# Causal and strict masks of two attentions: added by VectorE on the diagonal block, or by an identity product on TensorE

## The chip, the cores and the metric

The kernel runs on one core of one Trainium2 chip. Its time is the device time of one execution in microseconds; a comparison takes the median of several executions. Everything is computed in fp32.

## The reference, cut to what matters

Two transformer blocks follow each other on 512 tokens of width 1024. The first block (windowed attention, convolution, a mixture of experts) is not touched. The second block has two attentions of 8 heads of 64, a projection, and a layer that gathers 128 rows of a table of experts for each token (8 heads, 16 experts a head):

```python
def forgetting_attention(q, k, v, log_fcum):          # "fox"
    ...
        logits = jnp.einsum('bhqd,bhkd->bhqk', qb, k, ...) * scale
        logits = logits + fq[..., :, None] - log_fcum[..., None, :]
        mask = k_pos[None, :] <= q_pos[:, None]
        logits = jnp.where(mask, logits, -jnp.inf)
        p = jax.nn.softmax(logits, axis=-1)

def stick_breaking_attention(q, k, v):                # "stick"
    ...
        mask = k_pos[None, :] < q_pos[:, None]
        log_beta = jax.nn.log_sigmoid(z)
        log_one_minus = jnp.where(mask, jax.nn.log_sigmoid(-z), 0.0)
        rest = lax.cumsum(log_one_minus, axis=3, reverse=True) - log_one_minus
        a = jnp.where(mask, jnp.exp(log_beta + rest), 0.0)

def peer_layer(h, w_query, sub_keys, expert_down, expert_up):
    ...
        u = expert_down[eb]
        act = jax.nn.gelu(jnp.einsum('td,thkd->thk', xb, u), approximate=False) * gb
        vv = expert_up[eb]
        return jnp.einsum('thk,thkd->td', act, vv)
```

## The kernel before

Each engine has its own program, written out by hand, and semaphores tie them together. The 512 queries are four tiles of 128. A unit `n` of an attention is one head and one tile `t` (`unit(n)`), over the keys of tiles 0 to `t`, so a unit works on 128 x `(t + 1) * 128` scores. There are 32 units of each attention. Units 0 to 7 are tile 0 of the eight heads ("the first part"); units 8 to 31 are tiles 1, 2, 3 of each head ("the second part").

The first part runs between the projections of the second block (`project2`, matmuls of L1969 and L1975): eight stick units, then eight fox units, one beside each projection. Then tile 0 goes through the output projection, the norm and its query, and the first top-16 selections are made.

The second part runs beside the expert layer. That layer is 32 steps (tile by head) of 8 parts; a part has two dot products of gathered rows on VectorE (`dot`, L1918), a piece of the top-16 selection for two steps later (`topk_part`), gelu and scaling on ScalarE (`coefs`, L1316 and L1318), and sums on TensorE (`up_sums`, L2595). GpSimd issues one gather for each of 16 experts a step (L885); a gather waits for its buffer (`pair_free`, given by TensorE after `up_sums`), and there are 8 buffers in the first 8 steps and 11 after. The list `PLAN` lays the attention's steps (`attend(s)`) behind the parts of the first six steps, in the same order on all engines, with 6 steps ahead of the first part. Stick units come first, then fox units, then output norm (`out_norm`), output projection, norm and queries of tiles 1 to 3. From step 8 on only the expert layer runs.

A stick unit: TensorE makes scores in a bank (`stick_scores`, L2436), ScalarE makes the softplus part `x` (`stick_soft`, L1177 to L1179), VectorE makes `x`, `y` and zeroes `x` on and above the diagonal (`stick_beta`, L1726, L1727, L1729, the last giving `sbb_done`), TensorE sums `x` over later keys into the same bank (`stick_sums`, L2444 and L2446) and adds the strict mask `stick_neg` there with a product of `ident` (L2448, giving `sbr_pe`), VectorE adds the bank to `y` (`stick_rest`, L1736), ScalarE takes the exponential, TensorE multiplies with the values (`stick_out`, L2460).

A fox unit: TensorE makes scores (`fox_scores`, L2392), adds the keys' decay (L2393) and adds the mask `causal` with a product of `ident` (L2394, giving `s_done`); VectorE takes the maximum (`fox_max`, L1750 and L1751), ScalarE the exponential (`fox_exp`, L1214), TensorE transposes (L2402), ScalarE copies (`fox_T`, L1223), TensorE multiplies with the values (L2412).

Both masks are 128 x 128 fp32 tiles in SBUF. A matmul of 128 x 128 fp32 stands in the trace as two rows. `link` on VectorE makes each of its instructions wait for the one before to be done.

Of the kernel before, what the change touches and what calls it, by code (L numbers as in the profile page):

```python
# [21 lines left out]
ALU = mybir.AluOpType  # L22
# [3 lines left out]
P = 128  # L26
# [6 lines left out]
H = 8  # L33
# [46 lines left out]
def build(nc, A, out):  # L80
    with ExitStack() as ctx:
        def sb(name, shape, dt=F32):
            return ctx.enter_context(nc.sbuf_tensor(name, shape, dt))

        def sem(name):
            return ctx.enter_context(nc.semaphore(name))
# [5 lines left out]
        bank = [ctx.enter_context(nc.psum_tensor(f"bank{i}", [P, 512], F32)) for i in range(8)]  # L92
# [24 lines left out]
        ident = sb("ident", [P, P])  # L117
        before = sb("before", [P, P])
        ones = sb("ones", [P, P])
        later_neg = sb("later_neg", [P, P])  # L120
        ones_neg = sb("ones_neg", [P, P])
        causal = sb("causal", [P, P])
# [6 lines left out]
        stick_neg = band_t[:, :, :].rearrange("p a b -> p (a b)")  # L129
# [124 lines left out]
        fcumT = arena_w[0:H, 4352:4352 + T]  # L254
# [135 lines left out]
        s_done = sem("s_done")  # L390
# [197 lines left out]
        def unit(n):  # L588
            return (n, 0, 0) if n < H else ((n - H) // NT[1], 1 + (n - H) % NT[1], 1)
# [9 lines left out]
        def stick_bank(n):  # L599
            return bank[1 + n % 3] if n < H else bank[(1, 2, 3, 7)[n % 4]]  # L600
# [37 lines left out]
        def slab(n):  # L638
            return slot(n % RING, *slabs[n][1])
# [737 lines left out]
        def _(dve):  # L1377
            link = Link(dve, dve_step)
# [340 lines left out]
            def stick_beta(n):  # L1719
                h, t, part = unit(n)  # L1720
                w = (t + 1) * P
                x, y, z = stick_x[part][n % 3], stick_y[part][n % len(stick_y[part])], stick_bank(n)
                dve.wait_ge(sbl_done, n + 1)
                if n >= len(stick_y[part]):
                    dve.wait_ge(sbo_pe, n + 1 - len(stick_y[part]))
                link(dve.scalar_tensor_tensor(out=x[:, 0:w], in0=z[:, 0:w], scalar=0.0, in1=x[:, 0:w], op0=ALU.max, op1=ALU.add))  # L1726
                link(dve.tensor_tensor(y[:, 0:w], z[:, 0:w], x[:, 0:w], ALU.subtract))  # L1727

                link(dve.tensor_tensor(x[:, t * P:w], x[:, t * P:w], before[:, :], ALU.mult), sbb_done)  # L1729

            def stick_rest(n):
# [6 lines left out]
            def stick_step(k, first):  # L1738
                part = int(first > 0)
                if of_part(k - REST[part], first):  # L1740
                    stick_rest(k - REST[part])
                if of_part(k - BETA[part], first):
                    stick_beta(k - BETA[part])

            def fox_max(n):
                w = (unit(n)[1] + 1) * P
                dve.wait_ge(s_done, H * TT + n + 1)
                if n >= 3:
                    dve.wait_ge(p_done, H * TT + n - 2)
                link(dve.tensor_reduce(smx[:, n % 3, 0:1], bank[1 + n % 3][:, 0:w], AX, ALU.max))  # L1750
                link(dve.tensor_scalar(smx[:, n % 3, 2:3], smx[:, n % 3, 0:1], -1.0, None, ALU.mult), nmax_done)  # L1751
# [11 lines left out]
            def fox_step(k, first):  # L1763
                part = int(first > 0)
                if of_part(k, first):
                    fox_max(k)
                if of_part(k - FOX_OUT[part], first) and last_of_head(k - FOX_OUT[part]):
                    fox_out(k - FOX_OUT[part])
# [196 lines left out]
        def _(pe):  # L1965
            def project(dst, w, at, rhs, chunks=DC, stationary=None):

                for c in range(chunks):
                    mm = pe.matmul(dst, w[:, c, at], rhs[:, c, :], start=(c == 0), stop=(c == chunks - 1))  # L1969
                return mm  # L1970

            def rows_of(dst, xT, t, w, at, chunks=DC):

                for c in range(chunks):
                    mm = pe.matmul(dst, xT[:, c, t * P:(t + 1) * P], w[:, c, at], start=(c == 0), stop=(c == chunks - 1))  # L1975
                return mm
# [28 lines left out]
            for c in range(DC):  # L2005
                if c % 2 == 0:
                    slab_ready(pe, N_MOD + c // 2)
                for j in range(4):
                    mm = pe.matmul(bank[0][32 * j:32 * j + 2, :], cvec[:, 0:2, c], slab(N_MOD + c // 2)[:, c % 2, T * j:T * j + T],
                                   start=(c == 0), stop=(c == DC - 1))  # L2010
# [7 lines left out]
            for c in range(DC):  # L2018
                for half in range(2):
                    mm = pe.matmul(bank[1][64 * half:64 * half + 64, 4 * c:4 * c + 4].rearrange("p (k r) -> p k r", k=2),  # L2020
                                   modr[:, c:T:DC], pick[:, :, 32 * half:32 * half + 2], start=True, stop=True)
# [36 lines left out]
            for m in range(18):  # L2058
# [6 lines left out]
                dst = bank[4 + m % 4]  # L2065
                if m < 4:
                    mm = project(dst[:, :], slab(N_K), slice(m * P, (m + 1) * P), hT)
                elif m < 8:
                    mm = project(dst[:, 0:CTX], slab(N_K), slice((m - 4) * P, (m - 3) * P), hcT)
                elif m < 10:  # L2070
                    mm = rows_of(dst[:, :], hcT, m - 8, slab(N_V), slice(0, 512))
                elif m < 14:
                    mm = rows_of(dst[:, :], hT, m - 10, slab(N_V), slice(0, 512))
                else:
                    mm = project(dst[:, :], slab(N_Q), slice((m - 14) * P, (m - 13) * P), hT)
                mm.then_inc(proj_done, 1)
                if m in PROJ_JOB:
                    j = PROJ_JOB.index(m)
# [50 lines left out]
            for i in range(PU + 3):  # L2129
# [10 lines left out]
                if i in AT_JOB:  # L2140
                    j = 3 + AT_JOB.index(i)
# [9 lines left out]
            for c in range(DC):  # L2151
# [9 lines left out]
                n = N_GA if c < 4 else N_GA + 4  # L2161
# [223 lines left out]
            def fox_scores(n):  # L2385
                h, t, part = unit(n)
                w = (t + 1) * P
                if n >= 3:
                    pe.wait_ge(p_done, H * TT + n - 2)
                at = slice(HD * (h % 2), HD * (h % 2) + HD)  # L2390
                dst = bank[1 + n % 3]
                pe.matmul(dst[:, 0:w], fqT[at, h // 2, t * P:(t + 1) * P], fkT[at, h // 2, 0:w], start=True, stop=False)  # L2392
                pe.matmul(dst[:, 0:w], ident[0:H, h:h + 1].broadcast_to([H, P]), fcumT[:, 0:w], start=False, stop=False)  # L2393
                pe.matmul(dst[:, t * P:w], ident[:, :], causal[:, :], start=False, stop=True).then_inc(s_done, 1)  # L2394

            def fox_transposes(n):
                h, t, part = unit(n)
# [18 lines left out]
            def fox_step(k, first):  # L2416
                part = int(first > 0)
                if k == first:
                    pe.wait_ge(sbc_done, UNITS if part else H)
                    pe.wait_ge(sbo_done, 1 + H if part else 1)  # L2420
                if of_part(k, first):
                    fox_scores(k)
                if of_part(k - FOX_T[part], first):
                    fox_transposes(k - FOX_T[part])
                if of_part(k - FOX_OUT[part], first):
                    fox_weighted(k - FOX_OUT[part])
# [13 lines left out]
            def stick_sums(n):  # L2440
                h, t, part = unit(n)
                x, dst = stick_x[part][n % 3], stick_bank(n)
                pe.wait_ge(sbb_done, n + 1)
                pe.matmul(dst[:, 0:(t + 1) * P], later_neg[:, :], x[:, 0:(t + 1) * P], start=True, stop=False)  # L2444
                for k in range(1, t + 1):
                    pe.matmul(dst[:, 0:k * P].rearrange("p (j q) -> p j q", q=P), ones_neg[:, :],  # L2446
                              x[:, k * P:(k + 1) * P].unsqueeze(1).broadcast_to([P, k, P]), start=False, stop=False)
                mm = pe.matmul(dst[:, t * P:(t + 1) * P], ident[:, :], stick_neg, start=False, stop=True)  # L2448
                mm.then_inc(sbr_pe, 1)

            def stick_out(n):
# [11 lines left out]
            def stick_step(k, first):  # L2463
                part = int(first > 0)
                if of_part(k, first):
                    stick_scores(k)
                if of_part(k - SUMS[part], first):
                    stick_sums(k - SUMS[part])
                if of_part(k - OUTS[part], first):
                    stick_out(k - OUTS[part])  # L2470
# [25 lines left out]
            for half in range(2):  # L2496
                pe.wait_ge(mixed_done, half + 1)
                for k in range(AC):
                    mm = pe.transpose(bank[1 + half][:, k * P:(k + 1) * P], mixed[0][half][:, 0, k * P:(k + 1) * P], ident[:, :])
# [144 lines left out]
            for n in range(TT * H):  # L2644
                t = n // H
# [53 lines left out]
```

## Time and profile before

| | us |
|---|---|
| median of 3 runs | 2970.42 |
| lowest and highest | 2962.66 and 2971.54 |
| the profiled execution | 2969.21 |
| its span, first to last instruction | 2967.4 |
| TensorE busy | 2264.3 (76%) |
| VectorE busy | 1420.9 (48%) |
| ScalarE busy | 758.9 (26%) |
| mean granted clock of TensorE, of full speed | 0.867 |

The page lists busy time, 40 slices of the span (about 74 us each), DMA queues, the chain of work that ended last and the costliest groups. PE is TensorE's matmuls, PEld its weight loads, DVE VectorE, ACT ScalarE, POOL GpSimd. In the views by window, "(x)" is a count of instructions, PEclk the granted clock as a share of 2.4 GHz, and DMA the busy share of 16 DMA engines. Times of the trace are us from the start of the span; L2394 is a line of the kernel.

### The profile page before, as it was taken

To read this page: it belongs to the slowest core of one execution; us is meant where nothing else is said; L and a number is where in the kernel's file an instruction comes from. 1 tells how busy PE (TensorE), PEld (TensorE's weight loads), DVE (VectorE), ACT (ScalarE), POOL (GpSimd) and SP (SyncE) were. 2 spreads that over 40 slices of the span, in tenths; PEclk is the share of its full clock that TensorE was granted. 3 is DMA by queue.
4 is the path that set the end of the run, shared out by engine and by line. 5 is a ranking of instruction groups with operands and counts; after the bars stand their busy time and mean duration, and the time that the engine had idled before them with its cause. 6 is when DMAs were issued, how large, how long until landed. Compare 5 with 4: busy or idle time off the path is not lost. (4 is left out here: it accounts for less than half of the span.)

```text
span 2967.4 us, 28984 instructions
## 1 busy us (share of the span) xinstructions
PE 2264.3 (76%) x9828; PEld 967.2 (33%) x9828; DVE 1420.9 (48%) x3332; ACT 758.9 (26%) x1753; POOL 591.3 (20%) x587
## 2 busy tenths in 40 slices
PE   5997899987777775799988978867755655565554
PEld 2543444532222222755655443322211111111110
DVE  2575411410000001301377667667678777777765
ACT  3104301110000001312177653222222222222212
POOL 0000000010000001000112223344344433443442
PEclk9999999989998997799998889888777777778786
DMA  9168429589999996512447868899999999999996
GB/s 340 60 240 291 167 79 211 206 318 400 404 402 399 398 399 245 182 57 84 147 175 288 307 262 320 359 411 416 417 421 422 421 421 421 421 404 421 421 421 253
DMA packets 213260, 922.17 MB, mean 311 GB/s; under 512 B 18986, under 2 KB 58968, under 8 KB 121230
## 3 DMA queue, kind: packets, MB, share of 16 engines
q0 software_dynamic: 78864, 552.72, 45.9%
q1 hardware_dynamic: 124480, 359.15, 33.0%
q10 hardware_dynamic: 9790, 8.73, 0.9%
q8 instruction: 65, 1.06, 0.1%
q14 instruction: 61, 0.50, 0.0%
HBM read 888.78 MB, written 31.77 MB: 310 GB/s over the span
## 5 line engine op out<-in xcount | busy, mean ns | idle before, releaser
L2595 PE MATMUL bank<-ring,arena_w 128*32 128x512 f32 x1568 | 604.1, 790 | 310.8 <-ACT arena_w L1318 310.6
L885 POOL DMA_INDIRECT ring<-in_expert_pair,ids x392 | 414.9, 1058 | 1048.6 <-PE bank L2595 680.1
L1969 PE MATMUL bank<-arena_h,ring 128*128 128x128 f32 (+2 forms) x1264 | 363.3, 448 | 10.3 <-DMA ring<-in_w_in 7.9
L2249 PE MATMUL bank<-ring,arena_h 128*64 128x512 f32 x1056 | 271.1, 672 | 88.0 <-DMA ring<-in_w_exp_up 83.2
L2595 PEld LDWEIGHTS bank<-ring,arena_w 128*32 128x32 f32 x1568 | 104.6, 128 | 657.6 <-ACT arena_w L1318 467.4
L1918 DVE CUSTOM_DVE_ANT_0 ring<-ring,arena_h 128x1024 f32<-128x1024 f32 x203 | 244.9, 1225 | 80.4 <-DMA ring<-in_expert_pair,ids 48.6
L1918 DVE CUSTOM_DVE_ANT_0 ring<-ring 128x1024 f32<-128x1024 f32 x189 | 229.6, 1224 | 79.7 <-DMA ring<-in_expert_pair,ids 71.3
L1969 PEld LDWEIGHTS bank<-arena_h,ring 128*128 128x128 f32 x1264 | 204.1, 196 | 160.3 <-issue 127.3
L1316 ACT ACTIVATE arena_w<-arena_w 128x2 f32<-128x2 f32 x256 | 51.8, 202 | 769.7 <-DVE arena_w L1918 769.3
L1641 DVE TENSOR_TENSOR arena_q<-arena_q,bank 128x256 f32<-128x256 f32 x32 | 13.5, 421 | 484.3 <-ACT arena_q L1060 484.3
L2249 PEld LDWEIGHTS bank<-ring,arena_h 128*64 128x64 f32 x1056 | 91.9, 155 | 264.9 <-issue 259.5
L2595 PE MATMUL bank<-arena_h,arena_w 128*32 128x512 f32 x200 | 131.3, 794 | 24.8 <-ACT arena_w L1318 24.8
L1318 ACT ACTIVATE arena_w<-arena_w 128x32 f32<-128x32 f32 x512 | 136.4, 313 | 8.4
L2262 PE MATMUL bank<-ring,arena_q 128*64 128x512 f32 x528 | 120.6, 598 | 19.9 <-DVE arena_q L1644 19.3
L2595 PE MATMUL bank<-pair_last,arena_w 128*32 128x512 f32 x140 | 97.3, 836 | 40.7 <-ACT arena_w L1318 40.7
L864 POOL DMA_INDIRECT arena_v<-ys_d,slot_i x8 | 8.9, 1106 | 564.8 <-SPq L716 554.5
L2595 PE MATMUL bank<-arena_v,arena_w 128*32 128x512 f32 x140 | 93.2, 804 | 31.8 <-ACT arena_w L1318 31.8
L1060 ACT ACTIVATE arena_q<-bank 128x256 f32<-128x256 f32 x32 | 12.3, 384 | 323.5 <-PE bank L2249 323.5
L1316 ACT ACT_TABLE_LOAD x63 | 80.8, 1283 | 50.6 <-DVE arena_w L1918 49.7
L1455 DVE SCALAR_TENSOR_TENSOR arena_x<-arena_x,convc 128x512 f32<-128x512 f32 x120 | 90.2, 752 | 4.3
L1975 PE MATMUL bank<-ring,arena_h 128*128 128x512 f32 x192 | 88.4, 618 | 0.0
L1524 DVE TENSOR_TENSOR arena_w<-bank,arena_w 128x512 f32<-128x512 f32 x8 | 8.3, 1036 | 154.8 <-ACT arena_w L1022 154.8
(472 smaller groups left out, 3040.8 us busy)
## 6 DMA issues: line engine op xcount, KB each, us to landing
ring<-in_w_exp_gate SPq DMA_DIRECT2D x33, 2048.0 KB, 19.4
ring<-in_w_exp_up SPq DMA_DIRECT2D x33, 2048.0 KB, 23.8
ring<-in_w_exp_down SPq DMA_DIRECT2D x33, 2048.0 KB, 24.9
ring<-in_w_in SPq DMA_DIRECT2D x15, 2048.0 KB, 20.2
ring<-in_w_mod SPq DMA_DIRECT2D x12, 2048.0 KB, 19.3
ring<-in_w_ada SPq DMA_DIRECT2D x12, 2048.0 KB, 14.7
xs_d<-zeros SPq DMA_DIRECT2D x1, 12032.0 KB, 70.8
ys_d<-arena_h ACTq DMA_DIRECT2D x64, 128.0 KB, 7.3
```

What stands on the lines that cost most here:

```text
L885: pool.indirect_dma_start(pair[pair_of(m)], None, A["expert_pair_2"], bass.IndirectOffsetOnAxis(ap=ids[n % 2][:, r:r + 1], axis=0)).then_i ...
L1060: act.activation(silu_g[b], bank[2 + b][:, 0:256], ACT.Silu).then_inc(silu_done, 1)
L1316: link(act.activation(gel[:, k0:k0 + count], dots[:, k0:k0 + count], ACT.Gelu))
L1318: act.activation(sel_q[:, n % 2, k, :], sel_q[:, n % 2, k, :], ACT.Copy, scale=gel[:, k:k + 1]).then_inc(sel_done, 1)
L1455: link(dve.scalar_tensor_tensor(out=conv[:, cc, :], in0=u_pad[:, cc, k:k + T], scalar=convc[:, cc, k:k + 1], in1=conv[:, cc, :], op0=ALU.m ...
L1641: dve.tensor_tensor(hid[b], silu_g[b], bank[2 + b][:, 256:512], ALU.mult).then_inc(hid_done, 1)
L1918: dve.tensor_tensor_reduce(buf, buf, h2_q[r % 4], 1.0, 0.0, ALU.mult, ALU.add, dots[:, r:r + 1]).then_inc(dots_done, 1)
L1969: mm = pe.matmul(dst, w[:, c, at], rhs[:, c, :], start=(c == 0), stop=(c == chunks - 1))
L1975: mm = pe.matmul(dst, xT[:, c, t * P:(t + 1) * P], w[:, c, at], start=(c == 0), stop=(c == chunks - 1))
L2249: mm = pe.matmul(bank[2 + b][at, :].rearrange("p (g f) -> p g f", g=2), xbT[b][:, c, :], gu[:, :, c, 256 * half:256 * half + 256], start=( ...
L2262: mm = pe.matmul(bank[6 + b][CAP * j:CAP * j + CAP, :], hidT[b][:, k, CAP * half:CAP * half + CAP], slab(n)[:, half, k, 512 * j:512 * j + ...
L2595: mm = pe.matmul(bank[4 + 2 * (n // H % 2) + half][at, :], sel_q[:, n % 2, k0 + j, :], pair[pair_of(m + j)][:, D + 512 * half:D + 512 * ha ...
```

## The change

The identity products L2394 and L2448 go. In their place VectorE adds `stick_neg` to the diagonal block of `y` in `stick_beta`, ahead of the multiplication that gives `sbb_done`, and adds `causal` to the diagonal block of the fox scores, in place in the bank, ahead of the maximum. The closing flag and the semaphore move to the last matmul that is left.

```diff
                 link(dve.tensor_tensor(y[:, 0:w], z[:, 0:w], x[:, 0:w], ALU.subtract))
-
+                link(dve.tensor_tensor(y[:, t * P:w], y[:, t * P:w], stick_neg, ALU.add))
                 link(dve.tensor_tensor(x[:, t * P:w], x[:, t * P:w], before[:, :], ALU.mult), sbb_done)
...
             def fox_max(n):
-                w = (unit(n)[1] + 1) * P
+                t = unit(n)[1]
+                w = (t + 1) * P
                 dve.wait_ge(s_done, H * TT + n + 1)
+                diagonal = bank[1 + n % 3][:, t * P:w]
+                link(dve.tensor_tensor(diagonal, diagonal, causal[:, :], ALU.add))
                 if n >= 3:
                     dve.wait_ge(p_done, H * TT + n - 2)
...
-                pe.matmul(dst[:, 0:w], ident[0:H, h:h + 1].broadcast_to([H, P]), fcumT[:, 0:w], start=False, stop=False)
-                pe.matmul(dst[:, t * P:w], ident[:, :], causal[:, :], start=False, stop=True).then_inc(s_done, 1)
+                pe.matmul(dst[:, 0:w], ident[0:H, h:h + 1].broadcast_to([H, P]), fcumT[:, 0:w], start=False, stop=True).then_inc(s_done, 1)
...
-                pe.matmul(dst[:, 0:(t + 1) * P], later_neg[:, :], x[:, 0:(t + 1) * P], start=True, stop=False)
+                mm = pe.matmul(dst[:, 0:(t + 1) * P], later_neg[:, :], x[:, 0:(t + 1) * P], start=True, stop=(t == 0))
                 for k in range(1, t + 1):
-                    pe.matmul(dst[:, 0:k * P].rearrange("p (j q) -> p j q", q=P), ones_neg[:, :],
-                              x[:, k * P:(k + 1) * P].unsqueeze(1).broadcast_to([P, k, P]), start=False, stop=False)
-                mm = pe.matmul(dst[:, t * P:(t + 1) * P], ident[:, :], stick_neg, start=False, stop=True)
+                    mm = pe.matmul(dst[:, 0:k * P].rearrange("p (j q) -> p j q", q=P), ones_neg[:, :],
+                              x[:, k * P:(k + 1) * P].unsqueeze(1).broadcast_to([P, k, P]), start=False, stop=(k == t))
                 mm.then_inc(sbr_pe, 1)
```

## Rows read from the trace of the kernel before

**Rows 1.** The page: span, busy time of TensorE, DMA share in 40 slices.

```profile
span 2967.4 us, 28984 instructions
...
PE 2264.3 (76%) x9828; PEld 967.2 (33%) x9828; DVE 1420.9 (48%) x3332; ACT 758.9 (26%) x1753; POOL 591.3 (20%) x587
...
DMA  9168429589999996512447868899999999999996
```

**Rows 2.** Windows by stage: the columns, then one line a stretch.

```profile
core 0: us, PE busy (x) PEld busy (x) DVE busy (x) ACT busy (x) POOL busy (x), PEclk, DMA share, GB/s
1252.00:1332.00 80.00, 80.00 (x292) 47.19 (x292) 8.34 (x30) 15.41 (x39) 0.00 (x0) 0.92 0.15 47
1332.00:1395.00 63.00, 63.00 (x228) 38.06 (x228) 4.78 (x17) 10.31 (x33) 0.00 (x0) 1.00 0.21 74
1395.00:1487.00 92.00, 82.64 (x497) 55.93 (x496) 31.10 (x100) 19.48 (x35) 7.52 (x8) 1.00 0.44 155
1487.00:1627.00 140.00, 124.28 (x714) 80.84 (x714) 110.24 (x254) 112.93 (x199) 32.13 (x30) 0.90 0.60 221
1627.00:1738.00 111.00, 108.31 (x470) 51.61 (x469) 68.22 (x183) 68.21 (x134) 24.71 (x26) 0.88 0.77 294
1738.00:1930.00 192.00, 150.83 (x643) 64.62 (x645) 133.44 (x303) 62.99 (x149) 59.11 (x55) 0.85 0.83 325
1930.00:2967.00 1037.00, 633.48 (x2804) 161.02 (x2796) 747.60 (x1803) 251.02 (x761) 425.37 (x394) 0.78 0.98 407
```

**Rows 3.** Chain that ended last: start us, us, what.

```profile
1751.75 0.37 DVE ring L1760
...
1798.05 12.33 DMA arena_h<-in_expert_pair,ids
```

**Rows 4.** TensorE timeline, 1245:1345: start us, us, engine, line, operation.

```profile
1264.14 0.39 PE L2448 MATMUL bank<-band_t,ident 128*128 128x128 f32 x2
1264.37 0.33 PE L2460 MATMUL bank<-arena_v,spare 128*128 128x64 f32 x2
...
1338.57 0.49 PE L2394 MATMUL bank<-causal,ident 128*128 128x128 f32 x2
1338.89 5.33 PE L1969 MATMUL bank<-arena_h,ring 128*128 128x384 f32 x16
```

**Rows 5.** Waits of VectorE, 1230:1400: us in total, times, longest us.

```profile
DVE spare L1736 <- PE bank L2448: 59.6, 8, 14.7
DVE smx L1750 <- PE bank L2394: 55.1, 8, 13.4
```

**Rows 6.** Groups of VectorE by form: count | busy us, mean ns | idle before.

```profile
L1492 DVE TENSOR_TENSOR bank<-bank,arena_w 128x128 f32<-128x128 f32 x8 | 2.4, 298 | 8.6 <-PE bank L2098 8.4
```

**Rows 7.** VectorE timeline, 1245:1345: two 128x128 operations in a row.

```profile
1255.46 0.29 DVE L1727 TENSOR_TENSOR spare<-bank,spare 128x128 f32<-128x128 f32 x1
1255.78 0.29 DVE L1729 TENSOR_TENSOR spare<-spare,before 128x128 f32<-128x128 f32 x1
```

**Rows 8.** Waits of VectorE, then of TensorE, 1487:1627.

```profile
DVE ring L1736 <- PE bank L2448: 7.3, 4, 3.4
DVE ring L1726 <- ACT ring L1179: 5.8, 7, 1.5
...
PE bank L2444 <- DVE ring L1729: 5.3, 5, 1.9
```

**Rows 9.** TensorE timeline, 1570:1600, at half clock.

```profile
1570.72 0.64 PE L2448 MATMUL bank<-band_t,ident 128*128 128x128 f32 x2
1571.15 0.95 PE L2460 MATMUL bank<-arena_v,ring 128*128 128x64 f32 x4
```

**Rows 10.** Waits of VectorE, 1627:1738.

```profile
DVE smx L1750 <- PE bank L2394: 31.1, 16, 6.7
```

**Rows 11.** Windows among the stick units: before and at a fall of the clock.

```profile
1553.00:1567.00 14.00, 11.55 (x92) 7.02 (x90) 13.42 (x31) 11.45 (x21) 6.00 (x5) 1.00 0.76 280
1567.00:1580.00 13.00, 12.72 (x48) 9.11 (x48) 7.45 (x20) 10.37 (x19) 0.93 (x1) 0.61 0.53 194
```

## The prediction

> **What bounds the kernel now.** I read the page first [rows 1]: TensorE is busy 76% of the span, but the digits of DMA stand at 9 for nearly the whole last third. So the share of busy time doesn't say what an edit in the attentions is worth, and I cut the span into stages [rows 2]. From 1930 to the end the DMA engines are busy 98% of the time: the gathers of the expert layer set the pace there, and nothing of the change lies in that stretch. What matters is at what time that stretch begins.
>
> Ahead of it, stage by stage [rows 2]:
> - 1252 to 1332, first part of stick, and 1332 to 1395, first part of fox: TensorE busy for all of 80.0 and all of 63.0 us, VectorE for 8.3 and 4.8. TensorE is the bound, without a gap.
> - 1395 to 1487: a chain of norm, output projection, query and first selections for tile 0, TensorE busy 82.6 of 92. The change touches nothing of it; it starts when TensorE is through with fox.
> - 1487 to 1627, 24 stick units beside the expert layer: VectorE busy 110.2 of 140 with 254 instructions, TensorE 124.3. Both near full, and tied to each other.
> - 1627 to 1738, 24 fox units: TensorE busy 108.3 of 111 (98%), VectorE 68.2 (61%).
> - 1738 to 1930: norms, projections and queries of tiles 1 to 3; DMA share 0.83.
>
> The chain that ended last [rows 3] goes from the last fox unit's scaling on VectorE at 1751.75 through output norm and projection into gathers at 1798 and on to the end. So the end of the fox units is on the path. Gathers can't run ahead of the attention by more than their 8 buffers, whose release is TensorE's; an attention that ends earlier or later moves the start of the DMA-bound stretch by as much. I take that transfer as one to one and keep its failure as a rival.
>
> **Part by part.** There are 32 units of each kind, 8 in the first part and 24 in the second.
>
> First part, removed. The stick mask product starts at 1264.14 and the next matmul at 1264.37: a slot of 0.23 us. The fox one starts at 1338.57 and the next at 1338.89: 0.32 us [rows 4]. That is at full clock; the mean clock of the two stretches is 0.92 and 1.00 [rows 2]. So 8 x 0.23 / 0.92 = 2.0 us and 8 x 0.32 = 2.6 us, all on an engine that is never idle: -4.6 us. Added: 8 + 8 operations on VectorE, which waits there for the mask products 59.6 and 55.1 us [rows 5]. That wait hides them, at nothing; without it they would cost 16 x 0.32 = 5.1. TensorE asks for these units' results a projection or two (5.3 us each [rows 4]) later. The stretch 1395 to 1487, with its weights loaded when TensorE frees their slots, moves up with it.
>
> The price of the additions. The stick one is a 128 x 128 TENSOR_TENSOR, all in SBUF, like L1729: start to start in such a row is 1255.78 - 1255.46 = 0.32 us [rows 7]. The fox one reads and writes a PSUM bank in place; the nearest row is L1492, 128 x 128 in place in a bank, 298 ns, against 291 ns for the usual one [rows 6 and 7]: 0.33 us with the gap. Each price is known well; what is open is on whose path it falls.
>
> The Trainium skill ("VectorE: DVE Perf Modes", section on the TRN2 errata) gives (N + 151) / 0.96 ns for an fp32 addition, so 291 ns for 128 elements, more than half of it fixed. By that page a small mask on VectorE is poor value, which speaks against the change; the row says the same 0.29 us, and the sums here already contain it.
>
> Second part, stick. Added: 24 x 0.32 = 7.8 us on VectorE. Bounds: all of it on the path (+7.8), or none, with the relief of TensorE, 24 x 0.23 / 0.90 = 6.1 us, coming through in full (-6.1). Which end is nearer? Instructions of VectorE take 110.2 us, and each is followed by a gap of some 0.03 us, so 254 x 0.03 = 7.6 more: 118 of 140, 84%, is VectorE working. It waits for L2448 only 4 times and for ScalarE's softplus 7 times [rows 8], and TensorE in turn waits for L1729, before which the new instruction is put, 5 times, 5.3 us. So VectorE is the nearer bound: 0.85 x 7.8 = 6.6, less the relief at the four places where it stood waiting for L2448, about 4 x 0.33 (between 0.23 and the 0.43 at half clock [rows 9]) = 1.3. That makes +5.3 us.
>
> Second part, fox. Removed: 24 x 0.32 = 7.7 us at full clock, over a mean clock of 0.88 it is 8.7 us, on an engine busy 98% of the stretch [rows 2]. Added: 24 x 0.33 = 7.9 us on an engine with 43 us to spare. But the addition stands in front of the maximum and of the dot products queued behind it on VectorE, which ScalarE and then TensorE's sums wait for. VectorE comes to the unit early and waits in 16 of 24 units, 31.1 us in all [rows 10]; in the other 8 it comes late, and there the addition delays what follows. Bounds: -8.7 (TensorE alone decides) and 0 (the two cancel in a loop TensorE, VectorE, ScalarE, TensorE). I take the whole gain less the eight late units, -8.7 + 8 x 0.33 = -6.1 us, nearer the first bound since TensorE hardly stands still.
>
> Sum: -4.6 + 5.3 - 6.1 = -5.4 us. The profiled execution took 2969.2, so 2963.8; it lay 1.2 below the median of 2970.4, so 2965.0 for a median.
>
> **The rivals.**
> 1. VectorE sets the pace in both stages of the second part: the stick units cost the full 7.8, and in the fox units TensorE's freed time turns into waits for the transposed copies. -4.6 + 7.8 + 0 = +3.2: 2973.6. For it: VectorE is in the loop of every unit. Against it: 31 us of waits among the fox units.
> 2. TensorE decides everywhere: -4.6 - 6.1 - 8.7 = -19.4: 2951. For it: TensorE has the larger busy time in each stage. Against it: VectorE's 84% among the stick units.
> 3. The gain is taken back before 1930. The stretch 1738 to 1930 has a DMA share of 0.83 and parts at DMA's speed; if the gathers there are already as late as the DMA makes them, an attention that ends 5 us earlier only waits longer. Change 0 to -1: 2970.
> 4. Slower: the clock. Among the stick units TensorE would have less to do and wait more. From 1567 to 1580 its granted clock was 0.61, and VectorE was busy 7.45 of 13 us, against 13.42 of 14 just before at 1.00 [rows 11]; that fall cost about 13 x 0.96 - 7.45 = 5.0 us. One more such fall eats the forecast's gain; with four more the time is -5.4 + 20 = +15: 2985. It decides from three (+9.6, above the line of slower). For it: TensorE already stands for VectorE 5 times there. Against it: the removed products are 6 of 124 busy us.
>
> The Trainium skill ("TensorE: Matmul & The Clock Gate", "HAM oscillation — how this bites in real kernels") says that waits between bursts of matmuls bring the clock down to half again; by that page the fourth rival would be the natural outcome of moving work off TensorE. The two windows agree that it happens here; how often it would after the change, no row tells.
>
> **How the numbers follow.** A measurement of this kernel tells some 0.3% (8.9 us) from no change. Chances: the forecast 0.45, rival 1 0.18, rival 2 0.12, rival 3 0.15, rival 4 0.10. Faster by over 8.9 us, below 2961.5: rival 2 and the lower edge of the forecast, 0.22. Slower, above 2979.3: most of rival 4, 0.08. The rest, 0.70, is within. The forecast's own range, with its stick term from +3 to +7.8, its fox term from -8.7 to -3 and a clock fall more or less, is 2958 to 2972. The range for 8 in 10 takes in rivals 1 and 3 and the near edges of 2 and 4: 2954 to 2977.
>
> **What would show it.** The first fox unit after should start some 2 us earlier, and the stretch that begins at 1395 some 4.6 us earlier, both with TensorE still without a gap. The first softplus of the second part to the last stick product should take about 5 us longer, with VectorE's busy time there up by 7.0 us and more waits for L1729's successor. The fox stretch of 111 us should be some 6 us shorter, with VectorE's wait for scores shrunk from 31 us towards 20. The final stretch should keep its 1037 us. Wrong would be: a stick stretch that is no longer (rival 2), a fox stretch that is no shorter (rival 1), a final stretch or the one before it longer by what the attention gained (rival 3), a mean clock in the stick stretch well below 0.90 (rival 4).

## The result, and the profile after

The change made the kernel slower: median 2980.57 us against 2970.98, 20 runs each, ratio 1.0032 with a 95% interval of 1.0018 to 1.0046 (+5 to +14 us). A second comparison on one chip, beside the first group of experiments, gave 1.0039 (1.0024 to 1.0055). The forecast was 2965 us.

The page of the kernel after, its span, busy times, granted clock and DMA share:

```profile
span 2982.3 us, 28812 instructions
...
PE 2275.6 (76%) x9700; PEld 964.5 (32%) x9700; DVE 1439.7 (48%) x3396; ACT 761.8 (26%) x1753; POOL 603.3 (20%) x587
...
PEclk9999999988898898799988879888777877777867
DMA  9168429489999996512447777899999999999996
```

TensorE issues 128 matmuls less (64 products, two rows each), VectorE 64 instructions more, and yet TensorE's busy time went from 2264.3 us [rows 1] up to 2275.6. Its mean granted clock went from 0.867 down to 0.859.

The span alone doesn't locate the loss: what lies ahead of the second block's attentions took 1232.1 us in one execution of before and 1248.3 in another. So I cut both traces at the same events: last normalised row of the second block, start of the output norm of tile 0, first expert ids (L1889 of before), last stick addition (L1736), output norm of tiles 1 to 3, first gather buffer in `arena_v` (about step 8). After, cut so (same columns as rows 2):

```profile
core 0: us, PE busy (x) PEld busy (x) DVE busy (x) ACT busy (x) POOL busy (x), PEclk, DMA share, GB/s
1241.10:1403.50 162.40, 161.63 (x642) 101.46 (x642) 21.24 (x72) 33.97 (x92) 0.00 (x0) 0.96 0.16 52
1403.50:1468.00 64.50, 57.26 (x280) 38.45 (x280) 20.36 (x62) 11.82 (x21) 0.00 (x0) 0.92 0.30 98
1468.00:1628.70 160.70, 139.35 (x795) 91.74 (x793) 120.60 (x303) 109.65 (x192) 35.85 (x34) 0.88 0.58 218
1628.70:1769.70 141.00, 129.45 (x576) 59.47 (x576) 91.87 (x244) 85.52 (x168) 34.89 (x35) 0.79 0.76 289
1769.70:1994.80 225.10, 172.47 (x734) 70.00 (x734) 149.91 (x344) 67.70 (x163) 77.01 (x70) 0.86 0.87 345
```

Before, cut at the same events (rows 2 had round instants in their place):

```profile
1232.10:1401.40 169.30, 168.66 (x674) 108.02 (x674) 16.48 (x56) 33.74 (x91) 0.00 (x0) 0.94 0.15 50
1401.40:1461.40 60.00, 52.77 (x281) 35.07 (x280) 20.38 (x62) 11.85 (x22) 0.00 (x0) 1.00 0.33 105
1461.40:1614.90 153.50, 138.68 (x841) 93.86 (x841) 113.40 (x278) 109.15 (x192) 34.81 (x34) 0.92 0.61 228
1614.90:1752.10 137.20, 128.11 (x626) 61.69 (x624) 84.58 (x220) 85.55 (x168) 34.80 (x35) 0.88 0.78 297
1752.10:1976.70 224.60, 173.94 (x734) 70.11 (x734) 150.07 (x345) 67.48 (x163) 74.52 (x70) 0.85 0.87 345
```

| stretch | before | after | forecast |
|---|---|---|---|
| first part and tile 0 (first two lines) | 229.3 | 226.9 | -4.6 |
| 24 stick units | 153.5, clock 0.92 | 160.7, clock 0.88 | +5.3 |
| 24 fox units | 137.2, clock 0.88 | 141.0, clock 0.79 | -6.1 |
| to step 8 | 224.6 | 225.1 | 0 |
| step 8 to the end | 990.7 | 987.5 | 0 |

From the last normalised row to the end before takes 1735.3 us and after 1741.2: +5.9. The fox units, which were to pay for the stick units, are longer too, and their granted clock is 0.09 lower.

The prices themselves were read rightly. Before, TensorE's timeline in the first part has 0.55 us from the start of L2444 to the start of L2460 and 0.74 us from L2393 to L1969, with the mask product in between [rows 4]:

```profile
1263.82 0.49 PE L2444 MATMUL bank<-spare,later_neg 128*128 128x128 f32 x2
...
1338.15 0.48 PE L2393 MATMUL bank<-arena_w,ident 8*128 8x128 f32 x2
```

After, the same pairs of lines stand 0.32 and 0.41 us apart, so the slots were 0.23 and 0.33 us:

```profile
1278.95 0.49 PE L2446 MATMUL bank<-spare,later_neg 128*128 128x128 f32 x2
1279.27 0.33 PE L2461 MATMUL bank<-arena_v,spare 128*128 128x64 f32 x2
...
1335.82 0.48 PE L2396 MATMUL bank<-arena_w,ident 8*128 8x128 f32 x2
1336.23 5.43 PE L1972 MATMUL bank<-arena_h,ring 128*128 128x384 f32 x16
```

and VectorE's groups by form show what the additions cost, 299 and 291 ns:

```profile
L1750 DVE TENSOR_TENSOR bank<-bank,causal 128x128 f32<-128x128 f32 x32 | 9.6, 299 | 82.3 <-PE bank L2396 81.4
...
L1728 DVE TENSOR_TENSOR ring<-ring,band_t 128x128 f32<-128x128 f32 x24 | 7.0, 291 | 0.8
```

### The profile page after: what moved, and what is told of

Read it like the earlier page. It is cut to its first block and busy times, and to the rows that moved or that the text cites. A ratio compares the mean times of both kernels' runs of the same rounds, so it can differ in the third digit from the quotient of the medians.

```text
span 2982.3 us, 28812 instructions
## 1 busy us (share of the span) xinstructions
PE 2275.6 (76%) x9700; PEld 964.5 (32%) x9700; DVE 1439.7 (48%) x3396; ACT 761.8 (26%) x1753; POOL 603.3 (20%) x587
## 5 line engine op out<-in xcount | busy, mean ns | idle before, releaser
L885 POOL DMA_INDIRECT ring<-in_expert_pair,ids x392 | 426.5, 1088 | 1042.4 <-PE bank L2596 678.4
L2252 PE MATMUL bank<-ring,arena_h 128*64 128x512 f32 x1056 | 280.4, 691 | 83.5 <-DMA ring<-in_w_exp_up 78.6
L1978 PE MATMUL bank<-ring,arena_q 128*128 128x512 f32 x176 | 80.1, 612 | 4.8 <-DVE arena_q L1526 4.8
```

The costliest lines, as they stand in the source:

```text
L885: pool.indirect_dma_start(pair[pair_of(m)], None, A["expert_pair_2"], bass.IndirectOffsetOnAxis(ap=ids[n % 2][:, r:r + 1], axis=0)).then_i ...
L2252: mm = pe.matmul(bank[2 + b][at, :].rearrange("p (g f) -> p g f", g=2), xbT[b][:, c, :], gu[:, :, c, 256 * half:256 * half + 256], start=( ...
```

## The experiments

A comparison of times here has an interval of about 0.2% (6 us) to either side, while lengths of stretches repeat more closely. All lengths are between the events named above. Stick units 8 to 31 took 153.5 to 154.6 us in the eight profiles whose kernel has them as before, and fox units 8 to 31 took 136.3 to 137.6 us in five. I compare with 154.1 and 136.9 us. Where the first part has its products, that stretch with tile 0 took 229.3 to 231.8 us in nine profiles. So each kernel is judged by its stretches, and the times are given beside them. Each experiment has one profile, and some edited stretches came out differently in kernels that share the edit; this is said where it happens.

**e4_before and e3_after, controls.** No edit.

> The kernel before, unchanged, as a control: ratio 1.000 within 0.2%, and a second profile that shows how much the granted clock and the length of each stretch differ between two executions of one program. Both theories: clock 0.86 to 0.92 in the stretches of the second part, ends of stretches within 5 us of the first profile.

> The change itself once more, beside the others on one chip, and a second profile of it. Both theories: 7 to 12 us slower than before (1.003). If the clock of 0.78 among the fox units is the change's, it shows again, below 0.82; if that was one execution's, it lies near 0.88 and the fox stretch is shorter by some 8 us than in the first profile of it.

Measured: before against itself 0.9996 (0.9978 to 1.0015), after 1.0039 (1.0024 to 1.0055). The second profile of before, first part, tile 0, stick, fox:

```profile
1248.30:1414.40 166.10, 165.35 (x674) 105.64 (x674) 16.50 (x56) 33.78 (x92) 0.00 (x0) 0.96 0.15 51
1414.40:1478.70 64.30, 57.06 (x281) 38.26 (x280) 20.38 (x62) 11.83 (x21) 0.00 (x0) 0.92 0.31 98
1478.70:1632.80 154.10, 138.75 (x843) 94.21 (x841) 113.54 (x279) 109.10 (x192) 35.45 (x34) 0.92 0.61 229
1632.80:1769.40 136.60, 127.63 (x626) 62.19 (x624) 84.49 (x220) 85.50 (x168) 35.69 (x36) 0.88 0.78 297
```

and the second profile of after:

```profile
1234.50:1396.80 162.30, 161.52 (x641) 101.50 (x642) 21.21 (x72) 33.71 (x92) 0.00 (x0) 0.96 0.15 52
1396.80:1461.00 64.20, 56.96 (x281) 38.25 (x280) 20.36 (x61) 11.83 (x21) 0.00 (x0) 0.92 0.31 99
1461.00:1621.50 160.50, 139.08 (x795) 91.61 (x793) 120.57 (x303) 109.24 (x192) 35.88 (x34) 0.88 0.58 219
1621.50:1762.50 141.00, 130.27 (x576) 59.68 (x576) 91.93 (x244) 85.32 (x169) 34.50 (x35) 0.79 0.75 288
```

The stick and fox stretches of before are 154.1 and 136.6 us (153.5 and 137.2 in the first), those of after 160.5 and 141.0 (160.7 and 141.0), with clocks of 0.92, 0.88 and 0.88, 0.79 again. The lower clock belongs to the change, not to one execution: over the whole span it has a mean of 0.861 in the 20 executions of the change and in the 12 of e3_after, against 0.868 in the control's 12. The end points expected "within 5 us of the first profile" were 13 to 18 us off for the control; that comes from ahead of the attentions. From the last normalised row on it is 1737.1 and 1741.1 us: the change costs 4 to 6 us there.

**e1_no_masks, the removal alone.** The change without its two additions:

```diff
-                link(dve.tensor_tensor(y[:, t * P:w], y[:, t * P:w], stick_neg, ALU.add))
...
-                diagonal = bank[1 + n % 3][:, t * P:w]
-                link(dve.tensor_tensor(diagonal, diagonal, causal[:, :], ALU.add))
```

> The identity products of all 64 units are gone and nothing takes their place: this kernel leaves the masks of both attentions out. It is the removal alone. Theory 'VectorE pays': the added operations are what made the change slower (up to 64 x 0.32 = 20 us, some 15 on the path), the removal is worth something; then this kernel is 5 to 19 us faster than before (ratio 0.994 to 0.998). Theory 'clock': with fewer products TensorE falls to half clock more often, which eats what the removal gives; then it is within 3 us of before (0.999 to 1.001) and the granted clock of the second part's units is well under 0.90 and 0.88.

Measured: 1.0025 (1.0006 to 1.0045), so slower than before, outside what either theory gave. This kernel leaves both masks out. Its stick and fox stretches:

```profile
1464.50:1619.30 154.80, 135.64 (x795) 88.28 (x793) 113.78 (x278) 109.25 (x192) 34.16 (x34) 0.91 0.61 227
1619.30:1755.30 136.00, 125.39 (x576) 56.99 (x576) 84.80 (x220) 85.31 (x169) 34.54 (x36) 0.82 0.78 299
```

With 24 products a stretch less and nothing added, the stick units take 154.8 us (before 153.5 and 154.1) and the fox units 136.0 (137.2 and 136.6). TensorE's busy time times clock among the fox units, a rough measure of its work at full clock, is 125.4 x 0.82 = 102.8 us, against 128.1 x 0.88 = 112.7 in before. So the work did go away (some 10 us by this measure, 7.7 by the slots), the clock fell from 0.88 to 0.82, and about 1 us was left of the gain. From the last normalised row to the end this kernel takes 1737.1 us, like the control; the 7 us of the times above that are not seen in the profile.

**e2_both, the addition alone.** Before, with the two additions in `stick_beta` and `fox_max` and the products kept.

> VectorE adds the masks and the identity products stay as well (each mask counts twice, which changes no output). It is the addition alone, with TensorE's work as before. Theory 'VectorE pays': 14 to 16 us slower than before (1.005), slower than the full change by the 5 us or more that the products cost. Theory 'clock': 3 to 8 us slower than before (1.001 to 1.003) and no slower than the full change, with a granted clock in the second part near the 0.90 and 0.88 of before.

Measured: 1.0042 (1.0025 to 1.0058), as slow as the change and between the two theories. Stick and fox:

```profile
1465.90:1627.70 161.80, 142.44 (x840) 96.60 (x841) 120.52 (x303) 109.05 (x192) 36.34 (x34) 0.89 0.57 213
1627.70:1779.50 151.80, 143.04 (x626) 70.00 (x624) 91.94 (x244) 85.56 (x169) 35.38 (x36) 0.78 0.72 272
```

The additions cost 7.7 us among the stick units, the whole of 24 x 0.32. Among the fox units this profile has 14.9 us more, nearly twice 24 x 0.33, at a clock of 0.78 with the same work on TensorE as before (143.0 x 0.78 = 111.6). But the profiled execution took 2997.7 us, the longest of the kernel's eight, whose median is 2986.3. It holds a stretch at half clock of 20 us with TensorE busy throughout; in the fox units of the other profiles the longest such stretch is about 16 us (g1) and otherwise 6 to 7:

```profile
1696.00:1716.00 20.00, 20.00 (x84) 9.60 (x83) 8.77 (x20) 7.98 (x16) 1.87 (x2) 0.50 0.38 143
```

So the 14.9 us are not a price of the addition; g3_fox_both below gives that.

**f1_first_part.** Masks on VectorE for units 0 to 7 only.

```diff
+                if n < H:
+                    link(dve.tensor_tensor(y[:, t * P:w], y[:, t * P:w], stick_neg, ALU.add))
...
+                product = not (n < H)
...
+                if product:
+                    mm = pe.matmul(dst[:, t * P:w], ident[:, :], causal[:, :], start=False, stop=True)
```

> Only units 0 to 7 of both attentions (the first part) have their masks on VectorE; units 8 to 31 keep the identity products. Both theories: the stretch from the last normalised rows to the first expert ids is 2.5 to 4.5 us shorter than the 229.3 and 230.4 of before, and everything after it is as before; time 0.1% shorter than before. A rival says that the fall of the clock that stands between fox's first part and the first ids (64.3 against 60.0 us in two profiles of before) comes each time when the products are gone and takes all of it: then 229 to 230, and no change.

Measured: 1.0011 (0.9996 to 1.0027). First part and tile 0 take 227.9 us, stick 154.5, fox 137.6. The seven profiles of kernels that took the products out of the first part read 226.5 to 228.3, against 229.3 to 231.8 in the nine with them. So the gain is real and 1 to 5 us, 1.4 and 2.5 us for this kernel against the two profiles of before, at or below the lower end of what was expected. It is too small to show in the times.

**f2_stick_second and f3_fox_second, one attention each.** As f1, with `n >= H` in place of `n < H` for stick alone, and for fox alone.

> Only the second part's stick units (8 to 31) have their mask on VectorE, the rest is as before. Stretch from the first ids to the last stick sum: 153.5 and 154.1 in before, 160.7 and 160.5 with the change. Theory 'VectorE's time is the path': +6 to +7 us at a granted clock of 0.91 or more. Theory 'clock': +6 to +7 us, with the clock down to 0.88 as in the change, from half-clock stretches behind lengthened waits of TensorE. The fox units behind it: 137 us and 0.88 if each stage stands for itself, near 141 and 0.79 if the fox units inherit the state.

> Only the second part's fox units have their mask on VectorE. Stretch from the last stick sum to the output norm: 137.2 and 136.6 in before, 141.0 twice with the change. Theory 'clock': 139 to 143 us, granted clock 0.78 to 0.82 though TensorE has 24 products less. Theory 'inherited from stick': 128 to 133 us at 0.87 or more, the 6 us gain that was forecast. Time against before: +1 to +4 us by the first, -4 to -8 by the second.

Measured: 1.0021 (1.0001 to 1.0040) and 1.0026 (1.0006 to 1.0046). Stick and fox stretch of f2, then the fox stretch of f3:

```profile
1464.80:1625.50 160.70, 139.36 (x795) 91.65 (x793) 120.67 (x302) 109.21 (x192) 35.19 (x34) 0.88 0.58 218
1625.50:1762.60 137.10, 128.33 (x624) 63.97 (x624) 84.38 (x220) 85.36 (x169) 35.80 (x36) 0.86 0.78 297
```

```profile
1623.70:1763.80 140.10, 130.64 (x578) 59.89 (x576) 91.99 (x244) 85.48 (x168) 34.86 (x36) 0.79 0.75 290
```

The stick units alone give the whole +6.6 of the change; the fox units behind them keep 137.1 us. The fox units alone give 140.1 us at 0.79, 3.2 more than before, against 4.1 more in the change. Each stage stands for itself, and the fox units inherit 1 us at most.

**f4_late_add, the order.** The strict mask behind the multiplication that releases TensorE:

```diff
-                link(dve.tensor_tensor(y[:, t * P:w], y[:, t * P:w], stick_neg, ALU.add))
                 link(dve.tensor_tensor(x[:, t * P:w], x[:, t * P:w], before[:, :], ALU.mult), sbb_done)
+                link(dve.tensor_tensor(y[:, t * P:w], y[:, t * P:w], stick_neg, ALU.add))
```

> The change with one order turned round: the strict mask is added to y behind the multiplication that releases TensorE's sums, not ahead of it. VectorE's work is the same, TensorE is released 0.32 us earlier in each stick unit. Theory 'TensorE's longer wait for the multiplied x': the stick stretch comes back to 154 to 157 us from 160.6. Theory 'VectorE's own time': it stays at 159 to 161. The fox stretch stays at 141 by both.

Measured: 1.0014 (1.0000 to 1.0028). Stick 158.7 us at 0.90, between the two theories and just under the 159 at which the second began. Releasing TensorE earlier gives back 2 of the 6.6 us. The fox stretch was to stay at 141 and took 138.9 us at 0.80, though its edit is that of the change: with f3 that makes 141.0, 141.0, 140.1 and 138.9 us for one edit of the fox units, a spread of 2 us that is not explained.

**g1_double_fox, more work on TensorE.** Before, with the product of the causal mask issued twice in units 8 to 31.

```diff
+                if n >= H:
+                    pe.matmul(dst[:, t * P:w], ident[:, :], causal[:, :], start=False, stop=False)
                 if product:
                     mm = pe.matmul(dst[:, t * P:w], ident[:, :], causal[:, :], start=False, stop=True)
```

> Before, with the identity product of the causal mask issued twice in the second part's fox units (8 to 31); VectorE as before. Stretch from the last stick sum to the output norm, 136.6 to 137.6 in four profiles without an edit there. Theory 'time of TensorE': 24 x 0.32 us at 0.88 are added, 145 to 146 us at 0.87 to 0.89. Theory 'the clock follows what TensorE does': more dense work holds the clock up or leaves it, so the length grows by less than 4 us, with a granted clock of 0.88 or more.

Measured: 1.0005 (0.9979 to 1.0030). The fox stretch:

```profile
1628.70:1768.90 140.20, 132.85 (x674) 68.03 (x672) 84.52 (x220) 85.61 (x169) 35.81 (x36) 0.88 0.77 291
```

A product more costs 140.2 - 136.9 (mean of before's two) = 3.3 us at a clock of 0.88, less than half of what 24 slots come to (24 x 0.32 / 0.88 = 8.7). That is what the second theory gave.

**g2_fox_filler and g3_fox_both.** g2 is f3 with the product's work put back behind the semaphore, into a bank of the expert layer, where it adds zero; g3 is f3 with the mask product itself kept.

```diff
                 mm.then_inc(s_done, 1)
+                if n >= H:
+                    pe.matmul(bank[4][:, 0:P], ident[:, :], zeros[:, :], start=False, stop=False)
```

> The causal mask of units 8 to 31 on VectorE as in the change (stick as before), and in the place of the removed product, but behind the semaphore, a product of the identity with zeros into the expert layer's accumulating bank, which changes nothing there. TensorE's work is that of before, VectorE is released as early as in the change. Theory 'clock follows work': granted clock back at 0.86 to 0.90 and the stretch at or below 137 us (f3_fox_second: 140.1 at 0.79). Theory 'time of TensorE': 140.1 + 8 = 148 us at a clock of 0.79.

> The fox units 8 to 31 have both, product and addition, the stick units are as before: the addition alone on the fox stretch, without what e2_both inherits from its stick units. Theory 'the addition lengthens the loop and the clock falls with it': 149 to 152 us at 0.78 to 0.80, as in e2_both (151.8). Theory 'e2_both inherited it': near 140 us at 0.85.

Measured: 0.9996 (0.9973 to 1.0019) and 1.0028 (0.9999 to 1.0057). The fox stretch of g2, then that of g3:

```profile
1617.50:1755.00 137.50, 128.89 (x626) 62.60 (x624) 91.71 (x244) 85.51 (x168) 34.56 (x35) 0.86 0.78 296
...
1627.50:1767.80 140.30, 130.87 (x626) 64.13 (x624) 92.06 (x244) 85.56 (x169) 35.43 (x36) 0.85 0.76 288
```

In g2 TensorE does 7.7 us more than in f3, and the stretch is 2.6 us shorter, 137.5 against 140.1, with the clock at 0.86 against 0.79. With the product ahead of the semaphore (g3) it is 140.3 us at 0.85, the number of the second theory: the addition beside a kept product costs 3.4 us by itself. What that theory calls inherited is not shown, as f2's fox units inherited nothing from stick units as long. The fox units of g3 and e2_both are the same code and the same work for TensorE (130.9 x 0.85 = 111.2 us and 111.6); e2_both's are 11.5 us longer with the 20 us at half clock in them. Where 20 us at half clock stand in place of 10 at full clock, 10 us are lost, an estimate that gives nearly all of the difference. Why that execution had such a stretch is not known.

**h1_stick_filler, h2_first_and_filler, h3_change_fillers.** Fillers behind `sbr_pe` in the stick units of f2 (h1); f1 and g2 together (h2); the change with late addition and both fillers (h3).

> As f2_stick_second (strict mask of units 8 to 31 on VectorE, fox as before), with a filler product of identity and zeros behind the semaphore of each of those units' sums. Stretch from the first ids to the last stick sum: 154 in before, 160.7 at 0.88 in f2_stick_second. Theory 'clock follows work here too': 155 to 157 us at 0.91 or 0.92. Theory 'VectorE is the path among the stick units': 160 to 163 us, whatever the clock.

> The first part's masks of both kinds and the second part's fox masks on VectorE, a filler product behind the semaphore in the second part's fox units, stick units 8 to 31 with their identity product as before. Both theories: first part 2.5 to 3.5 us shorter than before, stick stretch 154, fox stretch 137 to 138; 2 to 3 us faster than before in sum, which lies within the 0.3% that can't be told from no change.

> The change with the late addition of f4_late_add and a filler product behind both semaphores in units 8 to 31: TensorE's work is that of before, VectorE's that of the change. Theory 'clock': stick stretch 155 to 157 (f4_late_add: 158.7), fox stretch 137 to 138 (138.9); time within 2 us of before. Theory 'VectorE's time': 158 to 161 and 138 to 141, and 4 us or more slower than before.

Measured: 1.0046 (1.0024 to 1.0069), 1.0000 (0.9978 to 1.0022) and 1.0027 (1.0010 to 1.0044). The stick stretch of h1:

```profile
1464.70:1623.30 158.60, 138.76 (x841) 94.13 (x841) 120.75 (x302) 109.00 (x192) 35.24 (x34) 0.92 0.60 224
```

The clock comes back to 0.92, and 2.1 of the 6.6 us with it, again between the two theories; 4.5 stay at the clock of before and with TensorE's work as before, and I put them down to VectorE's additions. In h3 stick takes 158.0 us at 0.92 and fox 140.3 at 0.85, as the second theory said. h2 has 228.3, 154.6 and 139.8 us (fox at 0.85), where 137 to 138 was expected for fox. So the fillers brought the clock up in all three kernels that have them in fox, but the length came back to before's in g2 only; in h2 and h3 TensorE did the filler's work at the higher clock in the same time. A clock of 0.85 is not enough to give the fox units the length of before. None of these is faster than before by what can be measured.

## Why the prediction was wrong, point by point

- **What bounds the kernel.** Right as to the path, but the transfer "as one to one" is not shown. From the last normalised row, step 8 began 9.1 us later than before (753.7 against 744.6 us), and the end came 5.9 us later, since the last stretch took 987.5 us against 990.7. It took 987.5 us in f1 too, where step 8 was hardly late (746.8 us), so it isn't the lateness that shortens it; what does is open. Rival 3 (a gain taken back before 1930) was not tested, as there was no gain to take back.
- **First part, -4.6.** Direction right, size 2 to 4 us. The slots were as read; the first part alone went from 166.1 us in the control to 162.3 in e3, -3.8, both at 0.96 with 64.3 and 64.2 us for tile 0 behind it. Other kernels with the same first part took 163.9 and 164.0 us. The first profile of before had 60.0 us over tile 0 at full clock, but 169.3 us at 0.94 ahead of it: the lower clock lay elsewhere, and the sum, 229.3, is only 1.1 below the control's.
- **Second part, stick, +5.3.** Right in kind, 1.3 too small: +6.6 (f2). Of it some 4.5 is VectorE's time on the path (h1) and about 2 the clock and the later release (f4, h1). The additions alone cost 7.7 us there (e2), the removal alone gave nothing (e1, +0.7). TensorE's waits for VectorE agree: after has 7.4 and 6.7 us where before had 2.8 for L1736 and 5.3 for L1729 [rows 8]; the first line is before's, the others are after's:

```profile
PE bank L2436 <- DVE ring L1736: 2.8, 4, 2.1
...
PE bank L2438 <- DVE ring L1736: 7.4, 4, 3.2
PE bank L2446 <- DVE ring L1729: 6.7, 6, 2.2
```

- **Second part, fox, -6.1.** This is the step that failed: "over a mean clock of 0.88 it is 8.7 us, on an engine busy 98% of the stretch". I divided the removed work by the clock of before and kept that clock for what is left. Measured, the removal alone gave 1 us in place of 8.7 (e1), with the clock down at 0.82. The other term, 8 x 0.33 = 2.6 us for the addition, was a little small: beside a kept product it cost 3.4 us (g3), and on top of the removal 3 to 5 (138.9 in f4, 140.1 in f3 and 141.0 in after, against 136.0 in e1). Together the stretch grew by 4 us, with the clock at 0.79. The 98% was read from a cut too narrow as well: 1627 to 1738 leaves out 26 of the stretch's 137 us, and between the events TensorE was busy 128.1 of 137.2 us, 93%. VectorE's wait for scores, which I expected to shrink from 31 us [rows 10] towards 20, hardly moved (26.7 us in the second profile of after, 28.4 in the control). In the first profile of after it was:

```profile
DVE bank L1750 <- PE bank L2396: 30.8, 14, 7.7
```

Had the remaining 129.45 x 0.79 = 102.3 us of work run at 0.88, TensorE would have been busy for 116 us in place of 129. That is an estimate of what the lower clock took, and it is more than the 8.7 us on which the forecast counted. In time at half clock, as the clock has two levels, the fox stretch had 2 x 0.12 x 137.2 = 33 us before and 2 x 0.21 x 141.0 = 59 after. Whether the stretch would have been shorter by so much at the old clock no run shows: where fillers brought the clock back to 0.85 or 0.86, they brought their own work too.
- **Rival 4, the clock.** This is the mechanism that I gave 0.10, and I looked for it in one place only. I priced falls of the clock among the stick units alone, where TensorE would wait longer. One such fall did come. Before, TensorE was busy 2.85 of the first 4 us here and kept full clock:

```profile
1505.40:1509.40 4.00, 2.85 (x18) 2.04 (x18) 3.32 (x7) 3.44 (x8) 0.00 (x0) 1.00 0.00 0
1509.40:1513.40 4.00, 3.13 (x52) 2.68 (x51) 2.14 (x7) 3.25 (x7) 0.00 (x0) 1.00 0.00 0
```

After, at the same place, it was busy 1.75 us of 4 and went to half clock (0.50). The second profile of after has the same fall, the control and h1 (with the filler) have none there. The last line is from among the fox units, where it is at half clock while busy all the time:

```profile
1512.00:1516.00 4.00, 1.75 (x12) 1.42 (x11) 3.83 (x10) 3.15 (x7) 0.00 (x0) 0.88 0.00 0
1516.00:1520.00 4.00, 4.00 (x8) 2.26 (x8) 1.62 (x5) 3.31 (x7) 0.00 (x0) 0.50 0.00 0
1704.70:1708.70 4.00, 4.00 (x16) 2.54 (x18) 3.77 (x7) 2.30 (x3) 0.00 (x0) 0.50 0.54 225
```

So a fall behind a longer wait is only one kind. Among the fox units the mean clock fell with hardly more waiting: TensorE was idle 9.1 us of 137.2 before at 0.88, 9.5 of 140.1 in f3 at 0.79 and 11.6 of 141.0 after. In the five profiles without these fox products and without a filler the clock is 0.79 to 0.82; in the eleven others, save e2_both's, it is 0.85 to 0.88. What makes it fall is not known.
- **Rival 1** (VectorE sets the pace in both, +3.2 in sum) gave the number that came nearest to what the profiles show (+4 to +6). Its mechanism holds for stick. Among the fox units the freed time did not turn into waits, as it says: they grew by 2.5 us at most.
- **What stays open.** The profiles show 4 to 6 us from the last normalised row on, the medians 9.6 and, on the second chip, 12.9 over before (intervals from 5 and 7 us). Whether the rest is chance, or lies ahead of the attentions, could not be told: that stretch differs by 16 us between two profiles of one kernel. The removal alone was also 7 us slower by the times and 0 to 2 by the profiles. Why the clock falls when products are taken out, why g2 and h2 differ by 2.3 us in the same fox units, and what another place of the fox addition would cost, no run shows.

## What to carry to other kernels

When TensorE is busy nearly all of a stage at a granted clock below 1, work taken off it may not be worth its duration: here the removal came back as a lower clock. Price such a removal between nothing and its slots, and take the middle only with a reason. And when a small operation moves between engines that wait for each other, ask what it costs the one that receives it: here 24 operations of 0.3 us on VectorE cost 4.5 to 7.7 us among the stick units and 3.4 among the fox units, and taking out the 24 products that they replaced was worth 1 us or less.

## What the runs showed of the hardware that I had not expected

- Work on TensorE that nothing waits for can raise its granted clock: a 128 x 128 product with zeros behind the semaphore of each fox unit took the clock from 0.79 to 0.86 (f3, g2), and to 0.85 in h2 and h3. The stretch went from 140.1 to 137.5 us in g2, but took 139.8 and 140.3 in h2 and h3. Among the stick units it went from 0.88 to 0.92 and 160.7 to 158.6 us (f2, h1).
- The mean clock of a stretch repeats from execution to execution (0.79 twice after, 0.88 twice before, among the fox units) though the stretch begins at another instant each time. It is not always so: TensorE was once at half clock for 20 us while busy all the time (e2_both), and that stretch was 11.5 us longer than the same units in g3.
- Doubling a product of 0.32 us in 24 units cost 3.3 us (g1), removing it gave 1 (e1).
